# Head norms spread through the delta rule, the mixing weights loaded there, and the start of attention regrouped

## The reference, cut to what matters

```
log_f = log_sigmoid(f_logit + b_f);  c = cumsum(log_f)
s = q k^T * scale + c_q - c_k;  causal mask;  softmax;  times v
```

```
ret = rmsnorm(ret) * silu(r_g)                 # no weight
dn  = rmsnorm(dn, dn_norm_w) * silu(d_z)       # weight of 128, the same for all heads
x   = x + gate1 * (concat(ret, dn) @ w_out)
```

## Time and profile before

| what | us |
|---|---|
| median of 3 runs (lowest, highest) | 3526.2 (3526.06, 3530.25) |
| the profiled execution | 3523.97 |
| its span | 3522.1 |
| TensorE busy in the span | 3103.1 (88%) |
| VectorE, ScalarE, GpSimd busy | 1535.7, 1125.4, 1110.3 |

### The profile page before, as it was taken

One profiled execution on the slowest core, in us unless ns is written; L12 is line 12 of the kernel. 1 busy time (PEld: TensorE's weight loads), 2 busy tenths in 40 slices (PEclk: granted clock), 3 DMA queues, 4 the chain that ended last, 5 costly groups with the idle time before them and its releaser, 6 DMA issues. The chain is left out here.

```text
span 3522.1 us, 40464 instructions
## 1 busy us (share of the span) xinstructions
PE 3103.1 (88%) x14608; PEld 2227.7 (63%) x14608; DVE 1535.7 (44%) x2012; ACT 1125.4 (32%) x1505; POOL 1110.3 (32%) x562
## 2 busy tenths in 40 slices
PE   6999999989999999769698997999594899999993
PEld 4666666468888788634343455999342677777772
DVE  4444444421111211336400334444415687878775
ACT  3333333011111122210210221222202677777773
POOL 1000110223333344400001213222000577878784
PEclk9999999999999999879799998999796899999996
DMA  2000001211111232145300004000303899999995
GB/s 86 24 25 19 25 25 59 91 47 52 50 48 48 77 119 93 57 185 179 146 24 23 30 31 174 13 13 1 124 9 123 286 372 371 368 368 375 365 375 214
DMA packets 116368, 450.06 MB, mean 128 GB/s; under 512 B 14609, under 2 KB 15569, under 8 KB 111265
## 3 DMA queue, kind: packets, MB, share of 16 engines
q1 hardware_dynamic: 103074, 396.83, 30.7%
q0 software_dynamic: 7856, 28.64, 2.4%
q10 hardware_dynamic: 5328, 23.07, 1.6%
HBM read 404.30 MB, written 44.10 MB: 127 GB/s over the span
## 5 line engine op out<-in xcount | busy, mean ns | idle before, releaser
L2685 DVE TENSOR_TENSOR moe_w_low<-moe_raw_up,moe_w_high 128x1024 fp32r<-128x1024 f32 x288 | 436.4, 1554 | 156.2 <-ACT moe_w_high L2625 156.2
L2548 POOL TENSOR_TENSOR moe_w_low<-moe_raw_down,moe_w_high 128x1024 fp32r<-128x1024 f32 x144 | 417.0, 2925 | 148.6 <-ACT moe_w_high L2635 148.6
L2625 ACT ACTIVATE moe_w_high<-moe_raw_up 128x1024 fp32r<-128x1024 f32 x288 | 304.9, 1062 | 187.5 <-PE ps L2588 110.3
L91 PE MATMUL ps<-x1T_high,w_up_high 128*128 128x512 f32 x704 | 274.7, 390 | 3.5 <-PEq L2906 3.5
L91 PE MATMUL ps<-x1T_low,w_up_high 128*128 128x512 f32 x704 | 274.3, 390 | 0.0
L91 PE MATMUL ps<-x1T_high,w_up_low 128*128 128x512 f32 x704 | 274.3, 390 | 0.0
L2603 PE MATMUL ps<-moe_w_high,moe_x_high 128*128 128x512 f32 x576 | 229.1, 398 | 4.2 <-DVE moe_x_low L2716 4.2
L2605 PE MATMUL ps<-moe_w_high,moe_x_low 128*128 128x512 f32 x576 | 226.0, 392 | 0.0
L2604 PE MATMUL ps<-moe_w_low,moe_x_high 128*128 128x512 f32 x576 | 225.6, 392 | 0.0
L764 POOL TENSOR_TENSOR w_up_high<-w_up,consts 128x1024 fp32r<-128x1024 f32 x44 | 83.5, 1897 | 382.7 <-PE ps L91 285.1
L272 POOL TENSOR_TENSOR qkv_low<-qkv_raw,qkv_high 128x1024 fp32r<-128x1024 f32 x22 | 53.6, 2436 | 468.3 <-ACT qkv_high L564 468.3
(11 more groups left out here) (433 smaller groups left out, 6147.4 us busy)
## 6 DMA issues: line engine op xcount, KB each, us to landing
moe_raw_up<-in_w SPq DMA_DIRECT2D x288, 512.0 KB, 10.2
moe_raw_down<-in_w SPq DMA_DIRECT2D x144, 512.0 KB, 9.1
w_ada<-in_w_ada SPq DMA_DIRECT2D x48, 512.0 KB, 4.6
w_up<-in_ffn_w_up SPq DMA_DIRECT2D x22, 1024.0 KB, 4.8
w_down<-in_ffn_w_down SPq DMA_DIRECT2D x44, 512.0 KB, 3.5
y_rows<-xT ACTq DMA_DIRECT2D x36, 512.0 KB, 8.2
qkv_raw<-in_attn_w SPq DMA_DIRECT2D x22, 512.0 KB, 3.5
y_rows<-zero_rows SPq DMA_DIRECT2D x1, 8192.0 KB, 29.1
```

The source lines that it names most:

```text
L91: ins = pe.matmul(out, stationary, moving, start=start and n == 0, stop=stop and n == last)
L2548: pool.tensor_tensor(w_low[:, down_slot(k)], raw_down[:, k], w_high[:, down_slot(k)].bitcast(F32), ALU.subtract).then_inc(down_low, 1)
L2625: act.activation(w_high[:, up_slot(n)], raw_up[:, n], ACT.Copy).then_inc(up_high, 1)
L2685: dve.tensor_tensor(w_low[:, up_slot(n)], raw_up[:, n], w_high[:, up_slot(n)].bitcast(F32), ALU.subtract).then_inc(up_low, 1)
```

## The change

- Attention: the forget logits are made one step of `k` earlier (after 2), the carry as well (after 5). The 24 DMAs are shared out: SyncE issues 8 as soon as the first part is there and 4 of the third part, ScalarE the 8 of the second part after its copies of q and k, GpSimd the other 4 of the third part. The pieces of unit 0 (24 matmuls) are made ahead of the wait for the DMAs.
- `stage_head_norm` is gone. Within the delta rule ScalarE squares and scales retention and squares the first six tiles of the delta rule, VectorE scales these six, GpSimd gates both. The squares go into `junk`, which is the tile `zeros`.
- The last two tiles of the delta rule (`LATE`) are normalized at the start of the mixing stage and transposed after its fourth product.
- `w_mix_out[1]` is loaded into the v part of `qkv` within the delta rule, `w_mix_out[0]` into `r_q` once all of retention is gated.

```diff
# stage_attention
+            sp.wait_ge(parted, 2)
+            for c in range(TILES):
+                spread_part(sp, 0, c, spread)
             sp.wait_ge(parted, 6)
-            for j in range(3):
...
+            for c in range(TILES // 2):
+                spread_part(sp, 2, c, spread)
# GpSimd: wait_ge(parted, 6), then spread_part(pool, 2, c, ...) for c in 2, 3
# ScalarE, after the copies of q and k:
+            act.wait_ge(parted, 4)
+            for c in range(TILES):
+                spread_part(act, 1, c, spread_act)
# TensorE
-                if k == 3:
+                if k == 2:
-                if k == 6:
+                if k == 5:
             pe.wait_ge(halves, 3)
-            pe.wait_ge(spread, 16 * 6 * TILES)
+            for n in pieces(0):
+                piece(0, n)
+            pe.wait_ge(spread, 16 * 3 * TILES)
+            pe.wait_ge(spread_act, 16 * 2 * TILES)
+            pe.wait_ge(spread_pool, 16 * TILES)
# stage_delta, SyncE
+            sp.dma_start(m.dn_norm_w[:], d["dn_norm_w"].partition_broadcast(P)).then_inc(w_loaded, 16)
...
+            for s in range(2):
+                sp.wait_ge(v_turned[s], CHUNK_PAIRS)
+            sp.dma_start(m.w_mix[1], d["w_mix_out"][1]).then_inc(m.mix_loaded[1], 16)
+            sp.wait_ge(r_gated, TT)
+            sp.dma_start(m.w_mix[0], d["w_mix_out"][0]).then_inc(m.mix_loaded[0], 16)
# stage_delta, GpSimd, in the last pair
+                    if i == LAST and level:
+                        gate_retention(level - 1)
+            for row in range(LEVELS - 1, TT):
+                gate_retention(row)
+            for row in range(EARLY):
+                pool.wait_ge(d_scaled, row + 1)
...
# stage_delta, VectorE
+            def scale_delta(row):
+                for h in range(MH):
+                    raw = m.qkv[:, h, row * P:(row + 1) * P]
+                    ins = dve.scalar_tensor_tensor(raw, raw, m.d_inv[:, row, h:h + 1], m.dn_norm_w[:],
+                                                   ALU.mult, ALU.mult)
+                ins.then_inc(d_scaled, 1)
...
+                    if i == LAST and level >= 3:
+                        scale_delta(level - 3)
...
+                if i == LAST:
+                    for row in range(LEVELS - 3, EARLY):
+                        scale_delta(row)
# stage_delta, ScalarE
+            def square_retention(row):
+                if row == 0:
+                    act.wait_ge(filled, 16)
+                else:
+                    act.wait_ge(r_squared, row)
+                for h in range(MH):
+                    ins = act.activation(junk[:, 0, h, :], m.r_norm[:, row, head(h)], ACT.Square,
+                                         accum_out=r_inv[:, row, h:h + 1])
+                ins.then_inc(r_squared, 1)
...
+            def beside_gate(i, n):
+                row = n // 2
+                if i == 0:
+                    square_retention(row)
+                if i == 2:
+                    scale_retention(row)
+                if i and row < 2:
+                    square_delta(2 * (i - 1) + row)
+                if i == 1 and n == 7:
+                    act.wait_ge(r_meaned, 1)
+                    act.activation(r_inv[:], r_inv[:], ACT.Sqrt).then_inc(r_rooted, 1)
+                if i == LAST and n == 7:
+                    act.wait_ge(d_meaned, 1)
+                    act.activation(m.d_inv[:, 0:EARLY, :], m.d_inv[:, 0:EARLY, :], ACT.Sqrt).then_inc(d_rooted, 1)
# every gate_copy(i, n) is followed by beside_gate(i, n)
# stage_mix_out, ScalarE, ahead of its copies
+            for j, t in enumerate(LATE):
+                for h in range(MH):
+                    ins = act.activation(junk[:, j, h, :], m.qkv[:, h, t * P:(t + 1) * P], ACT.Square,
+                                         accum_out=m.d_inv[:, t, h:h + 1])
+                ins.then_inc(squared, 1)
+            act.wait_ge(meaned, 1)
+            act.activation(m.d_inv[:, LATE[0]:, :], m.d_inv[:, LATE[0]:, :], ACT.Sqrt).then_inc(rooted, 1)
# stage_mix_out, TensorE
+            for t in range(LATE[0]):
+                turn(t)
             for i in range(NH * TT):
                 t, n = i // NH, i % NH
+                if t == 2 and n == 0:
+                    for late in LATE:
+                        turn(late)
+                if n == 0:
+                    pe.wait_ge(turned_out, t + 1)
+                if t == 0:
+                    pe.wait_ge(m.mix_loaded[n], 16)
```

More of the change, by code:

```diff
@@ L235, in wait_slot_free, with spread_part @@
                 eng.wait_ge(filled, through(of - 1, Q_HIGH if s == Q else K_HIGH))
+        def spread_part(eng, j, c, landed):
+            for head in range(2):
+                row = 64 * head + j
+                eng.dma_start(negc[row:row + 1, :, c * FCHUNK:(c + 1) * FCHUNK],
+                              parts[c * THIN + head:c * THIN + HEADS:2, j, :]).then_inc(landed, 16)
         @block.sync
@@ L276, in _ @@
             lower(V, 0, w_raw[:])
+            pool.wait_ge(parted, 6)
+            for c in range(TILES // 2, TILES):
+                spread_part(pool, 2, c, spread_pool)
             for p in range(1, PAIRS):
@@ L1713, in _ @@
                 after_half(3 * n + 2)
[L1716 to L1763, removed]
@@ L1803, in stage_delta @@
         zeros = sb("zero_rows", [P, D])
+        junk = zeros[:].rearrange("p (a h n) -> p a h n", a=2, n=MHD)
         wg = sb("w_gates", [P, 2, DT, GATE_COLS])
@@ L1887, in steps, with mean @@
                                   ).then_inc(stepped[s], 1)
+            def mean(ss, done):
+                dve.tensor_scalar(ss, ss, 1.0 / MHD, EPS, ALU.mult, ALU.add).then_inc(done, 1)
+            def scale_delta(row):
[4 more added lines that the diff above has]
+                ins.then_inc(d_scaled, 1)
             dve.memset(state[:], 0.0).then_inc(state_done, 1)
@@ L1995, in _ @@
                 gate_copy(i, 11)
+                beside_gate(i, 11)
                 for s in range(2):
@@ L2136, in sem @@
             return nc.alloc_semaphore(name)
-        w = m.qkv[:, 0:DT, :].rearrange("p c (b n) -> p (c b) n", b=NH).rearrange("p (a k) n -> p a k n", a=NH)
+        LATE = (TT - 2, TT - 1)
+        w = m.w_mix
+        junk = sb("d_norm_square", [P, 2, MH, MHD])
+        squared, meaned, rooted, inverted, scaled, d_gated = (sem("d_late_" + n) for n in (
+            "squared", "meaned", "rooted", "inverted", "scaled", "gated"))
         part = sb("mix_part", [P, 2, HALF])
-        loaded, turned, turned_out, summed, gated, added = (sem("mix_" + n) for n in (
-            "loaded", "turned", "turned_out", "summed", "gated", "added"))
+        turned, turned_out, summed, gated, added = (sem("mix_" + n) for n in (
+            "turned", "turned_out", "summed", "gated", "added"))
         mod_loaded, gate_loaded = sem("mix_mod_loaded"), sem("mix_gate_loaded")
@@ L2149, in _ @@
         def _(sp):
-            for n in range(NH):
-                sp.dma_start(w[:, n], d["w_mix_out"][n]).then_inc(loaded, 16)
             sp.dma_start(gate1, d["mod_row"][0, 2 * D:3 * D].partition_broadcast(P)).then_inc(gate_loaded, 16)
@@ L2161, in _, with turn @@
         def _(pe):
-            for t in range(TT):
+            def turn(t):
+                if t in LATE:
+                    pe.wait_ge(d_gated, t - LATE[0] + 1)
                 if t >= 2:
@@ L2185, in _ @@
         def _(dve):
+            late = m.d_inv[:, LATE[0]:, :]
+            dve.wait_ge(squared, 2)
+            dve.tensor_scalar(late, late, 1.0 / MHD, EPS, ALU.mult, ALU.add).then_inc(meaned, 1)
+            dve.wait_ge(rooted, 1)
+            dve.reciprocal(late, late).then_inc(inverted, 1)
+            dve.wait_ge(inverted, 1)
+            for j, t in enumerate(LATE):
+                for h in range(MH):
+                    raw = m.qkv[:, h, t * P:(t + 1) * P]
+                    ins = dve.scalar_tensor_tensor(raw, raw, m.d_inv[:, t, h:h + 1], m.dn_norm_w[:],
+                                                   ALU.mult, ALU.mult)
+                ins.then_inc(scaled, 1)
+            for j, t in enumerate(LATE):
+                gate = m.mixed[:, t, MW:2 * MW]
+                dve.wait_ge(scaled, j + 1)
+                dve.tensor_tensor(heads_of(gate), heads_of(gate), m.qkv[:, 0:MH, t * P:(t + 1) * P], ALU.mult
+                                  ).then_inc(d_gated, 1)
             for i in range(NH * TT):
@@ L2945, in second_block @@
         m.mixed = sb(s1, "mixed", [P, TT, D])
+        m.d_inv = sb(s1, "d_inv", [P, TT, MH])
+        m.dn_norm_w = sb(s1, "dn_norm_w", [P, MHD])
+        m.r_norm = rq
+        m.w_mix = [rq[:].rearrange("p a n -> p (a n)").rearrange("p (k n) -> p k n", k=DT),
+                   m.qkv[:, 2 * MH:3 * MH, :].rearrange("p c (b n) -> p (c b) n", b=NH)]
+        m.mix_loaded = [s1.enter_context(nc.semaphore(f"mix_loaded{n}")) for n in range(NH)]
         with nc.cleanup_on_exit():
```

68 lines of the change are left out of this document (53 added, 15 removed).

## The result

The changed kernel takes 3486.0 us (median of 4 executions, 3481.3 to 3488.3) against 3526.1 for the kernel before (3525.4 to 3530.3, 4 executions) on the same chip. The ratio is 0.9882, 95% interval 0.9868 to 0.9897: 40.1 us less. The forecast was about 3487. The execution that was profiled is the longest of the four (3488.32, span 3486.5; before 3523.97 and 3522.1), so the two spans lie only 35.6 apart.

A forecast was written before the change was run, and what follows sets the result against it. TensorE, busy 88% of the span, was taken as the bound, so a change pays only where it waits. 15 + 37.8 - 9.4 - 4 = 39.4 us off 3523.97 gives 3484.6, median about 3487; range 3475 to 3502.

The forecast's parts named there:

- attention: Attention stage: earlier forget sums and DMAs on three queues start the first scores at 46.6, not 56.4; 15 us gained.
- norm stages and mixing: Between delta rule and mixing: products start 39.8 us earlier, late transposes cost 2.0; net 37.8 us gained.
- the zeros: Delta rule's start: ScalarE's first square waits for the zeros' DMA, holding gate copies; 6.9 stall plus 2.5 clock, cost 9.4 us.
- port of GpSimd and VectorE: Delta rule's last pair: VectorE's fused multiplies wait for GpSimd at the common SBUF port; cost 4 us.
- Rival 1: Delta rule's start: the zeros cost nothing, landing sooner or absorbed by the gates; 3478 us, chance 0.12.
- Rival 2: Last pair's port costs 8, or small DMAs cost 1.5 us each on ScalarE and attention gives 9; 3497, chance 0.13.
- Rival 4: Norms not freed: GpSimd's gates come late and the stage waits for its tail; all 17.8 us exposed, 3505; chance 0.06.
- Rival 3: ScalarE becomes the delta rule's bound: all 88 squares and scales on TensorE's path, 48 us, 3535; chance 0.03.
- 1.4 us of room at n = 15: Delta rule: ScalarE's tightest place, ahead of the next pair's exponentials' table load; about 1.4 us of room, no cost.
- The waiting form: Last pair: three of four fused multiplies wait 1.07 us each for GpSimd's instruction; 4.4 us per group, price 4.
- the ratio: Last pair: fused multiplies slowed 2.6 times beside GpSimd; four take 3.0 us, hidden by room and slack, price 0.

The follow-up runs named there:

- e1: The kernel before with only the changed attention stage, all else as before: 3514.2 us, ratio 0.9961.
- e2: The changed kernel with attention as before, so only the norms moved: 3500.5 us, ratio 0.9919.
- e9: The changed kernel timed again, unchanged, in a later batch: 3482.6 us, ratio 0.988.
- e3: The changed kernel with a tile of its own for the squares' output, so ScalarE doesn't wait for the zeros' DMA: 3475.0 us, ratio 0.9847.
- e11: The changed kernel with GpSimd's eight retention gate multiplications cut to one column each: 3481.4 us, ratio 0.9875.
- e8: The changed kernel with the edits of e3, e4 and e5, and 12 added matmuls ahead of the first scores: 3478.4 us, ratio 0.9862.
- e5: The changed kernel with ScalarE's eight small DMAs of the forget sums moved to GpSimd: 3477.8 us, ratio 0.986.
- e6: The changed kernel with 12 added matmuls of 512 columns ahead of the first scores, into an unread bank: 3485.7 us, ratio 0.9887.
- e10: The changed kernel with four more 128x128 squares on ScalarE behind each of the delta rule's 32 gate copies: 3484.9 us, ratio 0.9877.
- e4: The changed kernel with all eight retention gates on GpSimd between the first and second level of the last pair: 3483.9 us, ratio 0.9871.
- e7: The changed kernel with the edits of e3, e4 and e5 together: 3467.5 us, ratio 0.9835.

## Why the prediction was right

**The sum.** Forecast 39.4 us less, measured 40.1. The terms, from the two profiles (35.6 between them) and from the runs:

| step | forecast | profiles | runs |
|---|---|---|---|
| attention | +15 (11 to 17) | +11.3 (+12.3 without the shift) | +14.0 (e1) |
| norm stages and mixing | +37.8 (35 to 40) | +41.1 to VectorE's first subtotal, -1.7 for the late transposes | 27.7 with zeros and port (e2) |
| the zeros | -9.4 (6 to 11) | -9.2 | -11.0, or -7.6 against e9 (e3) |
| port of GpSimd and VectorE | -4 (0 to 8) | -2.6 | -2.6 by the last pair's length (e11); by time not told apart |
| clock in the feed-forward stages | none | -3.3 | 1565.3 to 1571.3 in 13 profiles, e8 1577.3 |

All but the last term were named, and each lies in its range. The right total is partly luck. By the profiles attention was forecast 3.7 us too good, mixing 1.6 and the port 1.4 too poor, and 3.3 were lost at the lower clock in a part that the change doesn't touch; the sum of that is 35.6. The 40.1 of the medians come out only because the profiled execution was the longest of its four. Rivals 1, 2 and 4 are out: the zeros cost 9, a small DMA on ScalarE is issued in 0.75 us and not in 1.5, the port cost 2.6 and not 8, and GpSimd's last gate ends at 2476.0, 13 us ahead of the stage's end.

**Attention.** The regrouping did what was said: three queues instead of one, `V_LOW` as cover. The ends of the price of a small DMA on ScalarE were 0.40 and 1.0; it was 0.75. The term was sized too large in two places. First, the forecast took 1.2 us from the last issue to the scores, as with SyncE before; behind ScalarE's last issue it is 1.9 to 2.3 us in the seven profiles with this attention. TensorE stands idle for 2.5 to 2.9 us ahead of the scores, where the forecast's own times (44.8 to 46.6) leave 1.8. Second, the lower clock in the units behind it, named only in the range. The maximum of unit 1 comes at 51.70 where it came at 65.71, 15.0 earlier without the shift (forecast 15.8), but at the last scores only 12.3 of that is left. In e5, at full clock throughout, it is 18.6 and then 18.3. Over the seven profiles the lower clock lasts 3 to 14 us there, and attention is 3.3 us longer with the longest than with the shortest. e5 and e6 show the link from both sides: take the idle stretch away by an earlier issue or by dummy work, and the clock stays up.

**Norms and mixing.** 12.7 us after the last matmul, forecast 12. The squares were cheaper than the row of an exponential made them (0.29 against 0.36), the weights had landed, and the first product did not run at the lower clock as it had at the earlier trace rows. What the squares saved went to the transposes behind them: after a wait of 2.97 us they ran at 0.50 of the clock from 2496 to 2498, and three tiles took 4.48 us, where the forecast has 1.1 for each copy. Against the end of the delta rule the products start 39.3 us earlier (2537.09 to 2501.68, and 3.9 of shift), forecast 39.8. From there to VectorE's first subtotal are 7.2 us where it was 9.0: 1.8 that the forecast had at nothing. The late transposes cost 1.7, forecast 2.0.

**The zeros.** The chain was read right link by link, landing to square to copy to piece, and sized right. e3 shows it by removal. It is the change's largest loss, and it came from borrowing a tile that a DMA still reads.

**ScalarE** at no cost: e10 adds 29 us of squares and TensorE doesn't notice. Rival 3 is out by a wide margin; the stall of the zeros is one of order in its list, not of load. The forecast's estimate of 1.4 us of room at n = 15 was too small: with e10's squares 2.1 us stood there in two of the pairs, and no wait of TensorE came of it.

**The port.** The waiting form was the right one, not the ratio. A multiply of 0.27 takes up to 1.2 us beside an unbroken row of GpSimd's instructions of 1.3 us. The Trainium skill, "SBUF — State Buffer", section "Who interferes with whom", has the second of two such instructions wait for the whole of the first; the trace agrees, with 1.2 us against 0.27. The subtractions, with one operand in PSUM, keep their 0.67 beside the same masks. What tells the two forms apart is that the length of a group follows the number of GpSimd's instructions beside it: 1.13 us with none (e4), 3.2 with two masks (e11), 4.24 and 4.89 with two masks and the gates. A ratio of 2.6 would have given 3.0 each time. The price was 2.6 and not 4, because VectorE's waits end when GpSimd's row ends: the forecast had each of the four groups wait three times and take 4.4 us, but the first was through before the gate held it (3.17, as in e11 without gates) and the fourth took 3.22. Only the second and the third reached TensorE, with 0.27 and 1.30 us of waiting.

## What to carry to other kernels

Work on vectors goes from a stage where TensorE waits into one where it is busy nearly for free, if the engine that takes it has its place in the list behind nothing slow: here 29 us more of load cost nothing that shows, and one wait on a DMA cost 9. A scratch tile that a DMA still reads is not free; look for who waits behind the first writer. And small transfers belong on the queue that is free soonest: GpSimd could begin 3.6 us ahead of ScalarE, and with the clock that then stayed up this made attention 4 to 7 us shorter than in the seven profiles without it. For a gain of a few us compare the lengths of single stages, from one instruction to another that both kernels have: the 2.6 us of the last pair were exact to a few hundredths, while whole times spread over 8.

## What the runs showed of the hardware

- The stretch from attention's last scores to the delta rule took 1565.3 and 1571.3 us in two executions of one program, with TensorE's busy time 4.4 us apart through the length of its low-clock stretches. In 14 profiles such a stretch, less half of its time at the lower clock, was 1488 to 1492 us. Two whole times therefore don't settle a term of 3 us.
- A stop of 2.5 to 2.9 us ahead of thin matmuls was followed by a granted clock of 0.50 in all seven profiles that have it, for 3 to 14 us; with no stop (e5, e7) or with full matmuls in its place (e6) the same thin matmuls ran at 1.00.
- A small DMA is issued in 0.70 us by SyncE, 0.75 by ScalarE and 0.50 to 0.52 by GpSimd.
- VectorE's fused multiply 128x128 with three operands in SBUF: 0.27 us alone, in the mixing stage; 0.8 us beside two of GpSimd's masks (e11) and 1.2 beside GpSimd without a gap (the change).

```profile
2495.33 2.19 DVE L2290 SCALAR_TENSOR_TENSOR qkv<-qkv,d_inv,dn_norm_w 128x128 f32<-128x128 f32 x8
```
